# The last two experts of each mixture: results summed into their tokens on TensorE instead of through HBM, and the HBM rows read back earlier

## The reference, cut to what matters

```
expert_id, gate = router(x)            # two experts of 32 for each token, with their weights
for each expert e:                     # a block of the rows of its tokens
    h = silu(xb @ w_gate[e]) * (xb @ w_up[e])
    y = h @ w_down[e]
out[token] += gate * y                 # each token adds the rows of its two experts
h_next = norm(ALPHA * h + out)         # layer norm (third block: x + out, then the final RMS norm)
```

## Time and profile before

| what | us |
|---|---|
| median of 3 runs | 2155.4 (2151.24 to 2159.71) |
| the profiled execution, its own time | 2147.33 |
| its span in the trace | 2145.5 |
| TensorE busy | 1970.6 |
| VectorE busy | 678.6 |
| ScalarE busy | 404.3 |

### The profile page before, as it was taken

How to read it: one execution, slowest core, us unless ns; L and a number is a source line. 1 busy time by engine, 2 the same in 40 slices (tenths; PEclk the granted TensorE clock), 3 DMA queues, 4 the chain that set the end, 5 groups by cost and what they waited for, 6 DMA issues and landing times.

```text
span 2145.5 us, 25273 instructions
## 1 busy us (share of the span) xinstructions
PE 1970.6 (92%) x10013; PEld 1052.8 (49%) x10013; DVE 678.6 (32%) x1617; ACT 404.3 (19%) x873; POOL 119.2 (6%) x142
## 2 busy tenths in 40 slices
PE   8999989999999997799999999999499989999883
PEld 4444445555455453645545545544444445665442
DVE  0155547221111111535421111111637223532123
ACT  1033432111111111111111111111233222112112
POOL 0000001000000000000100000000010001111100
PEclk9999999999999999899999999999799999999997
DMA  9511103899999999722899999999821111699994
GB/s 318 152 57 40 40 20 114 356 419 420 420 421 421 420 419 372 273 83 79 313 419 420 421 420 421 421 419 404 287 84 40 39 40 41 217 366 418 419 419 200
DMA packets 122049, 593.93 MB, mean 277 GB/s; under 512 B 15915, under 2 KB 41403, under 8 KB 58991
## 3 DMA queue, kind: packets, MB, share of 16 engines
q1 hardware_dynamic: 108495, 565.96, 66.4%
q0 software_dynamic: 13472, 26.84, 3.8%
HBM read 573.48 MB, written 35.44 MB: 284 GB/s over the span
## 4 chain that ended last, share of the span: by engine, by line
PE 78%; DMA 14%; DVE 4%; ACT 2%; issue 1%; SPq 0%; DVEq 0%; POOLq 0%; ACTq 0%
PE bank L946 21%; PE bank L627 10%; PE bank L986 10%; PE bank L869 9%; DMA ring<-in_w_up_dram 6%; DMA ring<-in_moe_w_up_dram 6%; PE bank L769 4%; PE bank L639 4%; PE bank L613 3%; PE bank L1112 1%; PE bank L723 1%; PE bank L696 1%; PE bank L1073 1%; PE bank L860 1%; PE bank L683 1%
## 5 line engine op out<-in xcount | busy, mean ns | idle before, releaser
L946 PE MATMUL bank<-ring,work 128*64 128x512 f32 (+1 forms) x3008 | 562.5, 526 | 29.0 <-DMA ring<-in_w_up_dram 25.5
L946 PEld LDWEIGHTS bank<-ring,work 128*64 128x64 f32 x3008 | 224.8, 138 | 362.8 <-issue 335.3
L986 PE MATMUL bank<-ring,work 128*64 128x512 f32 x1280 | 295.9, 600 | 5.3 <-DVE work L1748 5.3
L1748 DVE COPY work<-bank 128x256 f32<-128x256 f32 (+1 forms) x96 | 36.5, 380 | 703.7 <-PE bank L861 703.7
L869 PE MATMUL bank<-work 128*128 128x128 f32 x2048 | 245.7, 278 | 0.0
L627 PE MATMUL bank<-hT,ring 128*128 128x512 f32 x512 | 236.9, 605 | 0.7 <-ACT work L1175 0.7
L869 PEld LDWEIGHTS bank<-work 128*128 128x128 f32 x2048 | 233.5, 192 | 6.1 <-issue 2.0
L1264 ACT ACTIVATE work<-bank 64x512 f32<-64x512 f32 x96 | 56.6, 589 | 540.8 <-PE bank L986 540.8
L986 PEld LDWEIGHTS bank<-ring,work 128*64 128x64 f32 x1280 | 84.3, 136 | 145.3 <-issue 129.1
L627 PEld LDWEIGHTS bank<-hT,ring 128*128 128x128 f32 x512 | 94.0, 193 | 109.1 <-issue 107.3
L1254 ACT ACTIVATE work<-bank 64x512 f32<-64x512 f32 (+1 forms) x96 | 49.7, 517 | 477.2 <-PE bank L946 477.2
(11 more groups left out here) (291 smaller groups left out, 1632.2 us busy)
## 6 DMA issues: line engine op xcount, KB each, us to landing
ring<-in_moe_w_down_dram SPq DMA_DIRECT2D x128, 1024.0 KB, 16.5
ring<-in_moe_w_gate_dram SPq DMA_DIRECT2D x126, 1024.0 KB, 15.4
ring<-in_moe_w_up_dram SPq DMA_DIRECT2D x126, 1024.0 KB, 17.2
ring<-in_w_down_dram SPq DMA_DIRECT2D x32, 1024.0 KB, 26.1
ring<-in_w_gate_dram SPq DMA_DIRECT2D x31, 1024.0 KB, 23.0
ring<-in_w_up_dram SPq DMA_DIRECT2D x31, 1024.0 KB, 24.9
ring<-in_attn_w_qkv_dram SPq DMA_DIRECT2D x12, 1024.0 KB, 13.7
work<-y_rows SPq DMA_DIRECT2D x12, 1024.0 KB, 8.0
```

What stands on the lines that cost most here:

```text
L946: mm = pe.matmul(GU2[s % 2][BLK * a:BLK * a + BLK, 0:F], xgT[pair % 2][:, per * kk + k, BLK * of_pair:BLK * of_pair + BLK], v[a][:, k, :], ...
L986: mm = pe.matmul(DN[BLK * n:BLK * n + BLK, :], hT_[:, 2 * kk + k, :], v[:, k, 512 * n:512 * n + 512], start=(kk + k == 0), stop=(2 * kk + ...
```

## The change

- Pair 15 (experts 30 and 31) is not stored: ScalarE copies its results to an SBUF tile `last_y`. VectorE multiplies the pair's selection matrix by the gates (`select_last`, in the slot of expert 27) and TensorE turns it (4 transposes, in the slot of expert 29, copied to `last_sum`). At the mixture's end TensorE multiplies `last_sum` with `last_y`, 2 matmuls of 128x512 for each tile of tokens (`sum_last_pair`), and VectorE adds the two banks to `h` (`add_last`). The gates of these rows are set to zero in the other sum (`elsewhere`).
- POOL stores 15 pairs. SP reads the four tiles as soon as pair 14's store has landed, and only then issues the next stage's first four weight buffers.
- In the first two mixtures the sums of tiles 0 and 1 go before the projection, those of tiles 2 and 3 behind the matmuls of tiles 0 and 1. VectorE adds tiles 0 and 1 from HBM first, then the banks. In the third mixture all sums are done at once.
- In the third mixture pair 15's input rows come by 64 matmuls instead of the indirect DMA and 8 transposes, since its selection matrix is now needed anyway.
- `y_rows` is zeroed at the start of the kernel, 4 MB more of writes ahead of those to `y_over`. The broadcast of a norm's gain at the end of the second mixture (L2040) waits for the last result copy.

```diff
@@ SP
+            sp.dma_start(y_rows.rearrange("(p n) (q c) -> p (n q) c", p=P, c=256),
+                         zeros[:, :].unsqueeze(1).to_broadcast([P, 2 * S // P * 4, 256])).then_inc(rows_zeroed, 16)
...
-                for y_stored in steps.y_stored:
-                    sp.wait_ge(y_stored, 16 * (E // 4) * (l + 1))
+                for y_stored, n in zip(steps.y_stored, STORES):
+                    sp.wait_ge(y_stored, 16 * n * (l + 1))
...
-            def after_gather(l, u0, u1):
+            def after_mixture(l, u0, u1, u2):
                 load_tiles(l)
+                for u in range(u0, u1):
+                    load(u)
                 for tt in range(T):
                     sp.wait_ge(routing.gathered[tt], 16 * (l + 1))
-                for u in range(u0, u1):
+                for u in range(u1, u2):
                     load(u)
@@ TensorE
+            def sum_last_pair(l, tt):
+                for n in range(2):
+                    mm = pe.matmul(last_bank(l, tt, n)[:, :], last_sum[:, P * tt:P * tt + P],
+                                   last_y[:, 512 * n:512 * n + 512], start=True, stop=True)
+                mm.then_inc(last_added, 1)
...
+                sum_last_pair(l, 0)
+                sum_last_pair(l, 1)
                 for tt in range(T):
                     turn(name, src, K, range(tt, tt + 1))
...
+                    if tt + 2 < T:
+                        sum_last_pair(l, tt + 2)
...
+                def turn_last_selection():
+                    pe.wait_ge(main.sel, main.sel0 + (4 if l == 2 else E // 2))
+                    for tt in range(T):
+                        mm = pe.transpose(XT[0][:, P * tt:P * tt + P], last_sel[:, tt, :], ident)
+                    mm.then_inc(main.xt, 1)
@@ ScalarE
-                    act.activation(ysb[s // 2][rows, 0:512], DN[0:BLK, :], ACT.Copy)
-                    act.activation(ysb[s // 2][rows, 512:D], DN[BLK:P, :], ACT.Copy).then_inc(main.ysb, 1)
+                    y = last_y if in_last else ysb[s // 2]
+                    act.activation(y[rows, 0:512], DN[0:BLK, :], ACT.Copy)
+                    act.activation(y[rows, 512:D], DN[BLK:P, :], ACT.Copy).then_inc(main.ysb, 1)
@@ VectorE
+            def add_last(l, tt):
+                dve.wait_ge(last_added, T * l + tt + 1)
+                for n in range(2):
+                    hs = h[:, tt, 512 * n:512 * n + 512]
+                    ins = dve.tensor_tensor(hs, hs, last_bank(l, tt, n)[:, :], ALU.add)
...
+                    for n in range(2):
+                        b = slice(BLK * n, BLK * n + BLK)
+                        ins = dve.tensor_tensor(last_sel[:, :, b], sel[1][:, :, b], over_last(gate_of[:, 2 * n, :], BLK),
+                                                ALU.mult)
+                    ins.then_inc(main.sel, 1)
+                    dve.tensor_tensor(wts, wts, elsewhere, ALU.mult)
...
             mixture(0)
-            combine_tile(0, 0, 0)
-            combine_tile(0, 0, 1)
+            for tt in range(2):
+                combine_tile(0, tt, 0)
+                combine_tile(0, tt, 1)
+            add_last(0, 0)
             tile_variance(0)
             for tt in range(T):
                 if 1 <= tt < T - 1:
                     combine_tile(0, tt + 1, 0)
                 tile_normal(tt, 1, tiles_written, turns["ffn0"].src0)
                 if tt + 1 < T:
-                    if tt == 0:
-                        combine_tile(0, 1, 0)
-                    combine_tile(0, tt + 1, 1)
+                    if tt:
+                        combine_tile(0, tt + 1, 1)
+                    add_last(0, tt + 1)
                     tile_variance(tt + 1)
@@ POOL
-                for q in range(E // 2):
+                for q in range(E // 2 - 1):
                     pool.wait_ge(main.ysb, main.n0 + 2 * q + 2)
```

More of the change, by code:

```diff
@@ L185, in at_mixture @@
             def at_mixture(self, l):
[L188 to L189 removed]
+                self.n0, self.x0, self.sel0 = E * l, (E + 1) * l, E // 2 * l
+                self.store0 = [16 * n * l for n in STORES]
         class Routing:
@@ L296, in wait_projected, with last_bank @@
                 eng.wait_ge(routing.projected, 2 * (T - 1) * l + 2 * tt + n + 1)
+        def last_bank(l, tt, n):
+            return bank[(4 + 2 * tt + n) % 8 if l == 2 else 4 + 2 * (tt % 2) + n]
         def turn_bank(name, tt, kk):
@@ L304, in turn_bank, with over_slots @@
             return bank[(2 * tt + kk) % 8]
[L306 to L312, removed]
+        def over_slots(eng, slot):
+            for s in range(TURN):
+                slot(0, s)
+            with eng.Fori(1, E // TURN - 2) as i:
                 for s in range(TURN):
                     slot(i, s)
-            for s in range(back * TURN):
-                slot(E // TURN - back + s // TURN, s % TURN)
+            for s in range(2 * TURN):
+                slot(E // TURN - 2 + s // TURN, s % TURN)
         def last_slot(i, s):
@@ L344, in gathered_pair @@
             if l == 2:
-                return type(i) is not int or 2 * i + c >= ONE_HOT
+                return type(i) is not int or ONE_HOT <= 2 * i + c < E // 2 - 1
             return False
@@ L977, in slot @@
                         turn_slots()
+                    if type(i) is int and j == E - 3:
+                        turn_last_selection()
                     pe.wait_ge(main.hT, main.n0 + j + 1)
@@ L1001, in mixture @@
                         turn_rows(m.ov, 0, 1, BLK)
-                        expert(m.ov, j, xgT[0][:, :, 0:BLK], 2 * j + 2, lambda q: ring[(m.base + q) % UNITS][:, :],
+                        expert(m.ov, j, xgT[1][:, :, 0:BLK], 2 * j + 2, lambda q: ring[(m.base + q) % UNITS][:, :],
                                lambda q: pe.wait_ge(m.ov_units, 16 * m.upb * j + 16 * m.upb))
+                    pe.wait_ge(m.ov.ysb, count)
+                pe.wait_ge(main.xT, main.x0 + E + 1)
+                pe.wait_ge(main.ysb, main.n0 + E)
+                if l == 2:
+                    for tt in range(T):
+                        sum_last_pair(l, tt)
             mixture(0, lambda k, tt: hT[:, k - 4, P * tt:P * tt + P])
-            project_turned("ffn0", h, first["pin"])
+            project_turned(0, "ffn0", h, first["pin"])
             u = first["pgrp"]
@@ L1020, in _ @@
             mixture(1, lambda k, tt: yT[k][:, P * tt:P * tt + P])
-            project_turned("rms0", hn, first["rec"])
+            project_turned(1, "rms0", hn, first["rec"])
             def bank_of(r):
@@ L1725, in overflow_and_weights, with select_last @@
                     link(dve.tensor_tensor(wts[:, 1, :], wts[:, 0, :], tokf[:, 36:40], ALU.mult))
+                def select_last():
+                    for n in range(2):
+                        for k in range(2):
+                            ins = dve.scalar_tensor_tensor(out=gate_of[:, 2 * n + k, :], in0=top_ids[:, k, :],
+                                                           scalar=float(E - 2 + n), in1=wts[:, k, :],
+                                                           op0=ALU.is_equal, op1=ALU.mult)
+                    link(ins)
+                    for n in range(2):
+                        ins = dve.tensor_tensor(gate_of[:, n, :] if n == 0 else gate_of[:, 2, :], gate_of[:, 2 * n, :],
+                                                gate_of[:, 2 * n + 1, :], ALU.add)
+                    link(ins)
+                    for n in range(2):
+                        b = slice(BLK * n, BLK * n + BLK)
[3 more added lines that the diff above has]
+                    dve.tensor_tensor(wts, wts, elsewhere, ALU.mult)
                 def expert(b, j):
@@ L1755, in slot @@
                         product(i, s + 1)
-                    if l < 2 and s % 2 == 0 and (type(i) is not int or 0 < j < E - 5):
+                    if s % 2 == 0 and (0 < j < E - 5 and (l < 2 or j == E - 6) if type(i) is int else l < 2):
                         select(s // 2, j + 4)
@@ L1761, in slot @@
                         overflow_and_weights()
-                over_slots(dve, l, slot)
+                    if type(i) is int and j == E - 5:
+                        select_last()
+                    if type(i) is int and j == E - 3:
+                        dve.wait_ge(main.xt, main.x0 + E + 1)
+                        dve.tensor_copy(last_sum, XT[0][:, :]).then_inc(main.xT, 1)
+                over_slots(dve, slot)
                 dve.wait_ge(routing.indices, m.l + 1)
@@ L1812, in _ @@
             mixture(1)
-            combine_tile(1, 0, 0)
-            combine_tile(1, 0, 1)
+            for tt in range(2):
+                combine_tile(1, tt, 0)
+                combine_tile(1, tt, 1)
+            add_last(1, 0)
             tile_variance(0)
@@ L1820, in _ @@
                 if tt + 1 < T:
-                    if tt == 0:
-                        combine_tile(1, 1, 0)
-                    combine_tile(1, tt + 1, 1)
+                    if tt:
+                        combine_tile(1, tt + 1, 1)
```

(9 more changed lines are left out.)

66 lines of the change are left out of this document (38 added, 28 removed).

## The result

The changed kernel takes **2162.15 us** (median of 20 runs, 2158.3 to 2174.67) against 2154.98 for the kernel before (20 runs in the same sessions): ratio 1.0032, 95% interval 1.0019 to 1.0045. That is 7.2 us slower, where 20.9 us faster was forecast. The profiled execution took 2163.03, its span is 2161.1. TensorE is busy for 43 us more (22.0 of them are the sums' rows) and stands still for 27 us less (147.6 instead of 174.9): waits were taken out, but more busy time came in than waiting went.

What follows compares the result with a forecast made beforehand. TensorE, busy 92% of the span, was taken as the bound, with standstills behind each mixture to win. Gains of 9.9, 9.0 and 2.0 summed to 20.9 us, from median 2155.4 to 2134.5, range 2125 to 2147.

Steps and rivals of the forecast that it cites:

- When the tiles come: First mixture: pair 14's store lands 8.4 us after issue, reads follow, tile 0 at 847.7, then one about every 2.5 us.
- To the projection: First mixture: tile 0's projection starts at 863.6, 11.6 us earlier, after 2.8 us for two adds; second mixture 11.7 earlier.
- The backlog: Rival: tile reads share engines with weights in flight, tile 0 6.1 us later in two mixtures; time 2146.7; chance 0.13.
- the read that isn't earlier: Rival: SP's wait ends only with the last expert, reads start at 850.2; gain about 4, time 2151; chance 0.07.
- the slower rival: Transfers behind the mixture, four tiles and two buffers, become the bound: 18 us slower, 2173; chance 0.03.
- Given back: First mixture: sums of tiles 2 and 3 cost 1.7 us; VectorE's loop, about 9.0, stays under TensorE's 9.4; net 9.9.
- What would show it: List of trace signs for right (earlier reads and projections) and wrong (late reads, TensorE waiting for buffers, VectorE late in slots).
- The second mixture's net of 9.0: Projection of tile 0 11.7 us earlier, VectorE sets two gaps at 10.3, last tile at 1549.5 against 1558.36.
- Loss first: Third mixture: pair 15's gather matmuls cost 2.6 us after savings in weight waits, between 0 and 3.9.
- Gain: Third mixture: tile 0 arrives 7.6 us earlier, four adds take 5.6, net 2.0.
- Costed at nothing: Zeroing of `y_rows`, extra slot work and reads ahead of next-stage buffers taken as covered; zeroing at most 25 us without cover.
- The chances: Main forecast 0.62, free third mixture 0.12, unseen 0.03; outcome faster by over 0.5% 0.85, within 0.5% 0.11, slower 0.04.

Runs made afterwards that it cites:

- the early-sum run: Changed kernel with the sums of tiles 2 and 3 ahead of the projections of tiles 0 and 1 in the first two mixtures: 2142.53 us, ratio 0.9946.
- all three edits and the fillers: Changed kernel with early sums, ScalarE's copy before the next root, third-mixture gather, plus 5 and 9 idle-bank matmuls in the first two mixtures: 2133.78 us.
- the run of all three edits: Changed kernel with sums ahead of projections, ScalarE's copy ahead of the next tile's root, and the third mixture's last pair by gather: 2137.56 us, ratio 0.9916.

## Why the prediction was wrong

**The gain, right.** *When the tiles come*: the reads were forecast 8.4 us behind the store's issue at once, tile 0 at 847.7, which with the 6.26 that the last down product lies later (851.53 against 845.27) is 853.96; VectorE starts on tile 0 at 853.95. *To the projection*: 11.6 and 11.7 earlier forecast, 10.7 and 11.9 measured. Without sums and adds the run gained 13.6 + 15.1 = 28.7; the forecast's gain before its own deductions was 11.6 + 2.8 and 11.7 + 2.8, 28.9. The backlog, the read that isn't earlier and the slower rival's transfers are ruled out: in the first mixture the reads went out at 849.05 and tile 0 landed 4.9 later, and TensorE never waits for weights in these tails.

**The step that failed is "Given back"**: "The sums of tiles 2 and 3 stand in TensorE's order between the tiles' matmuls, 4 x 0.43 = 1.7. VectorE's loop per tile grows by 1.4 to about 9.0, under TensorE's 9.4 (8.5 and 0.9), so it isn't the bound", and for the second mixture "10.3 for two gaps". It adds up each engine's own work and takes the largest. That holds only if the engines run side by side. Here tile 2's sum waits for tile 0's projection, tile 2's add and variance for the sum, tile 1's copy for tile 2's root, tile 1's projection for the copy: the period is the sum of the links, 9.74 + 1.73 + 4.17 = 15.64, which is the measured gap. The forecast named in "What would show it" TensorE waiting for buffers and VectorE being late in the slots, and not this wait. It cost 7.1 + 12.6 = 19.7 us by the distances; the early-sum run won 19.6 back by the medians.

**A second, smaller miss in the same step: the sizes.** The sum of one tile takes 1.73 in the chain, where 0.86 was forecast.'s L627 x64 was read as 64 matmuls, but the profile shows a 128x512 matmul in float32 as two rows: the two matmuls of a tile are "x4". So each takes 0.86 us, not 0.43. And the clock behind the wait wasn't in the sum at all: 3.7 for the sum ahead of the first projection. In a good order, sums and adds cost 7.6 + 8.3 = 15.9 instead of 4.5 + 5.5 = 10.0, 5.9 more. (The second mixture's net of 9.0 is 8.9 by its own starts, 1558.36 and 1549.5; it changes nothing.) The three pieces (0.2 of gain, 19.7, 5.9) make the 25.8 us between the forecast's 18.9 for the first two mixtures and the measured -6.9.

**The third mixture, nearly right.** *Loss first*: 2.6 forecast, within 0 and 3.9; gate 31 fell back by 19.9 where gate 28 had fallen back by 16.6, so 3.3. *Gain*: the tile lands 10.3 later than before in absolute terms, behind a gate 31 that is 19.9 later, thus 9.6 earlier, where 7.6 + 2.6 = 10.2 was forecast. From the mixture's first gate it is 6.0 earlier. The four adds: from the tile's landing to the end 24.65 instead of 19.3, 5.35 against 5.6. Net 6.0 - 5.35 = 0.7 instead of 2.0, a difference too small for one execution to be sure of. The rows are from the chain of waits at the end, which answers to the earlier trace rows:

```profile
...
2131.72 4.74 DMA work<-y_rows
...
2136.47 1.30 DVE h L1427
...
2141.76 0.70 DVE h L1436
```

**Costed at nothing, right.** The zeroing was, by the trace; the slots of the first two mixtures too: from the first gate to the last down product it took 466.4 us after (385.13 to 851.53) and 465.7 before in the first, 466.6 and 467.1 in the second. The four next-stage buffers behind the reads never kept TensorE waiting; VectorE waited 0.83 and 0.60 us for tile 1, where the forecast had it wait for nothing, and that may be theirs (not shown). The rule of the Trainium skill (DMA: Bandwidth & Descriptors, Where 436 GB/s comes from), a bind at about 358 GB/s between HBM and SBUF, wouldn't have saved the forecast: with it the estimate is 19 instead of 20.9. Nor does the trace bear the limit out. Tile 1 did land 3.4 us behind tile 0, where I took 2.5 and an estimate from the page's figure is 2.9, but in those 3.4 us 417 GB/s were moved in all, with the next stage's first buffers already behind it in the queue:

```profile
853.90:857.30 3.40, 2.03 (x9) 0.66 (x5) 2.57 (x2) 2.04 (x3) 0.00 (x0) 1.00 1.01 417
```

**The chances.** Slower had 0.04, on transfers that become the bound. (The 0.85 for faster is more than its parts give: 0.62 + 0.12 + 0.065 + 0.03 is 0.835.) The right slower case was in the code: two fixed orders that cross. It asked for one question on each wait that the change adds, who stands behind the waiting instruction, and for `add_last(2)` the answer was the variance whose root stood ahead of a copy.

## What to carry to other kernels

When a change puts a new producer into one engine's fixed order and its consumer into another's, follow the loop once around with the tile numbers written down: if the way back to the same engine carries tile t+1, the period is the sum of the links, not the largest engine's share. Put the new work ahead of the long work of the same turn, where its inputs are ready anyway; here the same matmuls gave 7 us of loss behind the projection and 12 us of gain ahead of it. The version with all three edits and the fillers beats both kernels, 21 us under the one before.

## What the runs showed of the hardware

- The clock: in the early-sum run TensorE's granted clock was full (2.4 GHz) from 850 to 855, where the first two sums end, 0.92 from 855 to 860 and at half (1.2 GHz) from 860 to 865; TensorE had waited 4.8 us, turned a tile in 1.8 and waited 3.6. Matmuls on idle banks kept it up in the first mixture and won 2.4 us; in the second, nine of them (7.89 us) kept it up over the turn and not over the sum behind it. The projection at 901.10 of the changed kernel ran at full clock behind a standstill of 3.31 us, the one at 886.40 didn't.
- In the first routing head the profiled executions differ where the kernels' code is the same. For 350 to 400 us the clock is 0.93 in the early-sum run, 0.86 in the changed kernel and 0.76 in the run of all three edits and the one with no sums, and these four have one head. The kernel before has 0.93, and 0.76 with the zeroing. At 0.76 the gates start some 10 us later than at 0.93. So two spans of one execution each can't be subtracted here; distances within a stage can, to about 2 us. What decides between the levels in that head isn't known.
